# Query and key blocks of two attentions computed with tokens on partitions: head norms by VectorE sums in place of TensorE matmuls with ones

## The chip, the cores and the metric

The kernel runs on one core of a Trainium2 chip. The metric is the device time of one execution in microseconds (us); shorter is better. Five engines work side by side, each through its own queue of instructions: PE (TensorE), DVE (VectorE), ACT (ScalarE), POOL (GpSimd) and SP (SyncE, which issues the weight loads). They are ordered against each other by semaphores alone.

## The reference

Two transformer blocks on 256 tokens of width 2048, all in fp32. What the change touches lies in the first block:

```python
def rms_norm(x, g):
    y = xf * lax.rsqrt(jnp.mean(xf * xf, axis=-1, keepdims=True) + NORM_EPS)
    return y * g
...
h = rms_norm(x, norm_g)
proj = h @ w_in                                     # split into aq, ak, av, az, B's columns, cq, cz, ga, gb, gc
aq = rms_norm(aq.reshape(bsz, s, 8, 128), a_q_g)    # over each head's 128 channels
ak = rms_norm(ak.reshape(bsz, s, 8, 128), a_k_g)
ya = chunked_band_attention(aq, ak, av, a_rel_bias) * silu(az)
yb = rwkv7_time_mix(br, bk, bv, ...) * silu(bz)
m = rms_norm(mem, mem_norm_g)
mk, mv = split(m @ w_mem_kv)
mk = rms_norm(mk.reshape(bsz, 256, 4, 256), c_k_g)  # over each head's 256 channels
cq = rms_norm(cq.reshape(bsz, s, 4, 256), c_q_g)
yc = memory_cross_attention(cq, mk, mv) * silu(cz)
merged = sigmoid(ga) * (ya @ w_up_a) + sigmoid(gb) * (yb @ w_up_b) + sigmoid(gc) * (yc @ w_up_c)
x = x + merged @ w_o
```

Four tensors get a norm per head: `aq`, `ak` (8 heads of 128 channels), `cq`, `mk` (4 heads of 256). The second block has another attention, a gated linear attention, a short convolution and a feed-forward part; the change doesn't touch it.

## The kernel before

**Units.** All weights stream through a ring. A block is 512 output columns of a weight matrix (or four, three or one groups of 128), and is cut into units of 128x1024 weights (512 KB): for each unit SP loads `w_raw`, ACT rounds it to fp32r (`w_hi`, `hi`, L622), DVE takes the rest (`w_lo`, `lo`, L1002), and PE multiplies (`unit`, from L1547). Each product is three matmuls: hi by hi, lo by hi, hi by lo. `RING = 4` units are in flight, and ACT and DVE work `LEAD = 3` units ahead of PE: at the place of unit n they do unit n + 3, ACT after PE has finished unit n - 1 (`unit_used`).

**Kinds.** In a "wide" block the weights stand in the array and the tokens stream: a unit has 2 x 4 x 3 = 24 matmuls of 256 columns (L1582 to L1584), and the result has channels on partitions. In a "rows" block the tokens stand and the weights stream: 2 x 2 x 3 = 12 matmuls of 512 columns (L1573 to L1575), and the result has tokens on partitions. Both end in the same two PSUM banks of `gp`, from which `evacuate` copies (ACT, L622 to L690) or merges (DVE).

**Order.** `plan_stream` (from L49) sets the order of the blocks for all engines: lora, B0, B1, then B2 B3 A0 A1, A2 B4 B5 A3, B6 B7 A4 A5, A6 A7, one gate block, then gate_b, C, gate_a, mem, gate_c, up_c, o and the second block. A0 to A7 are the columns of aq (0, 1), ak (2, 3), av (4, 5), az (6, 7); C0, C1 those of cq; the first two blocks of mem those of mk. Between the steps of all other work each engine calls `fill(k)`, which runs the next k units. While the RWKV pairs are computed (`pairs(g)`, `pair_begin(p)`, four joint steps of two pairs each, PE's small matmuls at L1745) the filler is counted in quarters of a unit by the table `STEPS` (`planned_quarters` on PE). A quarter is six matmuls of a wide unit or three of a rows unit.

**Head norms.** `heads_norm` is called in gate_b after two units (for a_q, a_k), in gate_a after two (c_q), in gate_c after three (c_k). The tensors lie with channels on partitions, four of the eight 128-channel tiles being a half. For each half ACT squares 1024 elements a partition (L765); PE adds over the channels and spreads the sum by four fp32 matmuls with a matrix of ones into `psCD` (L1687); ACT takes the root from PSUM (`root`, L614); DVE has four (or two) reciprocals of 256 elements (L1130) and four multiplications by gain and reciprocal (L1133); PE goes on with 6 (or 3) units. Then the next half follows, in the same buffers. `attention` begins when its norms are done (`hn_done`).

```python
for t in range(4):
    hd = t // per_head
    ins = pe.matmul(psCD[:, hd * T:(hd + 1) * T], ones[:], buf[:, t * T:(t + 1) * T], ...)
```

**Transposes.** `turn_rows` (L1630) turns 128x512 by two token halves in eight 128x128 transposes with `ident` into one of two PSUM pairs `cross`; it is used for the norms of rows and for the merged branches (`up_and_project`).

Of the kernel before, what the change touches and what calls it, by code (L numbers as in the profile page):

```python
# [8 lines left out]
ALU = mybir.AluOpType  # L9
# [43 lines left out]
def plan_stream():  # L53
# [90 lines left out]
def plan_fill():  # L144

    upto, n = {}, 0
    for p in range(-1, KB // 2):
        for step, quarters in FIRST_STEPS if p < 0 else STEPS:
            n += quarters
            upto[p, step] = n  # L150
    return upto
CROSS = {"norm_g": 0, "merged": 4, "norm1_w_2": 8, "merged_2": 12, "norm2_w_2": 16, "ffn": 20}


def build(nc, dram, out):
# [9 lines left out]
    with ExitStack() as ctx:  # L165
# [37 lines left out]
        small = sb("small", [P, 32])  # L203
        y_ctx = ExitStack()
# [84 lines left out]
        hn_sq, hn_rs = area(64, UNIT), area(68, UNIT)  # L289
# [7 lines left out]
        cq_sq, cq_rs = area(0, UNIT), area(4, UNIT)  # L297
        c_sq, c_rs = area(48, UNIT), area(52, UNIT)
# [74 lines left out]
        def planned(unit):  # L373

            todo = list(range(units_of("B2")[0], units_of("gate_b0")[-1] + 1))

            def fill(p, step):
                while todo and todo[0] - first_todo < upto[p, step] // 4:
                    unit(todo.pop(0))

            def drain():
                while todo:
                    unit(todo.pop(0))
            first_todo = todo[0]
            fill.drain = drain
            return fill

# [220 lines left out]
        def _(act):  # L608
# [15 lines left out]
            def evacuate(m):  # L624
# [6 lines left out]
                tiles = g.rearrange("p (a b) -> p a b", b=T)  # L631
                if kind == "lora":
# [13 lines left out]
                elif kind == "a_cols":  # L646
                    if a in (4, 5):
                        act.activation(piece(a_v, a - 4), halves(g), ACT.Copy).then_inc(done, 1)
                    else:
                        dst = {0: a_q, 1: a_k, 3: a_z}[a // 2][:, 4 * (a % 2):4 * (a % 2) + 4, :]  # L650
                        act.activation(dst, tiles, ACT.Silu if a >= 6 else ACT.Copy).then_inc(done, 1)
                elif kind == "c_cols":
                    dst = (c_q, c_z)[a // 2][:, 4 * (a % 2):4 * (a % 2) + 4, :]
                    act.activation(dst, tiles, ACT.Silu if a >= 2 else ACT.Copy).then_inc(done, 1)
# [6 lines left out]
                elif kind == "mem":  # L661
                    if a >= 2:
                        act.activation(piece(c_v, a - 2), halves(g), ACT.Copy).then_inc(done, 1)
                    else:
                        act.activation(c_k[:, 4 * a:4 * a + 4, :], tiles, ACT.Copy).then_inc(done, 1)
# [92 lines left out]
            def heads_norm(src, size, buf, rs, fill, fills, ready=lambda half: None):  # L758

                for half in range(2):  # L760
                    ready(half)
                    if act_n["hn"]:
                        act.wait_ge(sem("hn_sq_used"), act_n["hn"])
                    act_n["hn"] += 1
                    act.activation(buf, src[:, 4 * half:4 * half + 4, :].rearrange("p a b -> p (a b)"), ACT.Square,  # L765
                                   scale=size ** -0.5).then_inc(sem("hn_sq"), 1)
                    act.wait_ge(sem("hn_sq_used"), act_n["hn"])
# [99 lines left out]
            for src in (a_q, a_k):  # L867
                heads_norm(src, 128, hn_sq, hn_rs, fill, 6)
# [6 lines left out]
            heads_norm(c_q, 256, cq_sq, cq_rs, fill, 3, lambda half: wait_evacuated(act, phases["C"][0] + half))  # L875
# [27 lines left out]
            heads_norm(c_k, 256, c_sq, c_rs, fill, 3, lambda half: wait_evacuated(act, phases["mem"][0] + half))  # L903
# [79 lines left out]
        def _(dve):  # L983
# [141 lines left out]
            def heads_norm(dst, gain, per_head, rs, fill, fills):  # L1125
                for half in range(2):
                    seen.need("root_ready")
                    for hd in range(4 // per_head):
                        r = rs[:, hd * T:(hd + 1) * T]
# [4 lines left out]
                        if hd == 4 // per_head - 1:  # L1134
                            ins.then_inc(sem("hn_done"), 1)
                        fill(1)
                    fill(fills - 4 // per_head)
# [235 lines left out]
            heads_norm(a_q, "a_q_g", 1, hn_rs, fill, 6)  # L1373
            heads_norm(a_k, "a_k_g", 1, hn_rs, fill, 6)
# [7 lines left out]
            heads_norm(c_q, "c_q_g", 2, cq_rs, fill, 3)  # L1382
# [34 lines left out]
            heads_norm(c_k, "c_k_g", 2, c_rs, fill, 3)  # L1417
# [122 lines left out]
        def _(pe):  # L1540
# [138 lines left out]
            def heads_norm(per_head, buf, fill, fills):  # L1679
                for _ in range(2):  # L1680
                    seen.need("hn_sq")
                    if pe_n["hn"]:
                        pe.wait_ge(sem("hn_done"), pe_n["hn"])
                    pe_n["hn"] += 1
# [193 lines left out]
            heads_norm(1, hn_sq, fill, 6)  # L1878
            heads_norm(1, hn_sq, fill, 6)
# [7 lines left out]
            heads_norm(2, cq_sq, fill, 3)  # L1887
# [11 lines left out]
            heads_norm(2, c_sq, fill, 3)  # L1899
# [95 lines left out]
```

## Time and profile before

| | us |
|---|---|
| median of 3 runs | 3014.78 (3014.73 to 3018.39) |
| profiled execution, its own time | 3016.61 |
| its span, first to last instruction | 3014.9 |
| PE busy | 2960.3 (98%) |
| DVE busy | 1643.0 (54%) |
| ACT busy | 1336.8 (44%) |
| mean share of the DMA queue with the weights | 56.9% |
| granted TensorE clock, mean | 0.995 of 2.4 GHz |

How to read it: a bar of PE lasts from issue to the modelled end of a pipelined matmul, and bars of successive matmuls overlap, so what a matmul costs is the distance between two starts. PE "busy" doesn't mean that the array is full. The chain that ended last is followed back from the end of the kernel, at each step to what released the instruction or to the one before it on its engine; its entries on PE are distances, and can be added.

### The profile page before, as it was taken

The numbers are of one execution on the slowest core, as the hardware profiler recorded it, in microseconds if no ns is written. First come the engines' busy times: TensorE is split into PE (matmuls) and PEld (weight loads), VectorE is DVE, ScalarE is ACT, GpSimd is POOL, SyncE is SP. The second block draws the span as 40 slices with busy tenths as digits, with TensorE's granted clock in tenths as the row PEclk, the third lists the DMA queues.
The fourth block names the chain that finished last, engine by engine and source line by source line (L and its number), as shares of the span: only waits on it lengthen the run. The fifth ranks groups of instructions, "written<-read, shape, count | busy, mean of one in ns | idle before, by whom it ended". The sixth has DMA issues, their size and how long they took to land.

```text
span 3014.9 us, 44248 instructions
## 1 busy us (share of the span) xinstructions
PE 2960.3 (98%) x18994; PEld 2546.8 (84%) x18994; DVE 1643.0 (54%) x1882; ACT 1336.8 (44%) x1522; POOL 68.7 (2%) x173
## 2 busy tenths in 40 slices
PE   7999999999999999999999999999999999999998
PEld 7999988889989888798998789888888888888886
DVE  4565665675656466454554466554654444444444
ACT  4452443454554454444454444444444444444333
POOL 4000000001000000000000000000000000000000
PEclk9999999999999999999999999999999999999999
DMA  7343444566665655656566555666556666666554
GB/s 205 112 135 113 138 130 119 154 187 182 212 196 180 177 152 190 188 161 181 168 173 197 151 147 164 190 185 191 192 175 191 182 185 184 183 187 196 188 188 147
DMA packets 356184, 518.40 MB, mean 172 GB/s; under 512 B 18288, under 2 KB 137220, under 8 KB 355220
## 3 DMA queue, kind: packets, MB, share of 16 engines
q1 hardware_dynamic: 355220, 512.37, 56.9%
q0 software_dynamic: 768, 3.20, 0.4%
q8 instruction: 149, 2.44, 0.3%
q14 instruction: 47, 0.39, 0.0%
HBM read 513.39 MB, written 2.11 MB: 171 GB/s over the span
## 4 chain that ended last, share of the span: by engine, by line
PE 94%; DVE 2%; ACT 1%; issue 1%; POOL 1%; DMA 0%; SPq 0%; DVEq 0%; POOLq 0%; ACTq 0%
PE gp L1573 21%; PE gp L1574 21%; PE gp L1575 21%; PE gp L1582 8%; PE gp L1584 8%; PE gp L1583 7%; PE ps L1745 4%; PE ps L1630 1%; PE ps L1702 1%; PE ps L1733 1%; DVE w_lo L1002 1%; PE ps L1687 0%; POOL m_work L518 0%; ACT w_hi L622 0%; DVE arena L996 0%
## 5 line engine op out<-in xcount | busy, mean ns | idle before, releaser
L1002 DVE TENSOR_TENSOR w_lo<-w_raw,w_hi 128x1024 fp32r<-128x1024 f32 (+2 forms) x976 | 1168.0, 1204 | 998.1 <-ACT w_hi L622 995.2
L622 ACT ACTIVATE w_hi<-w_raw 128x1024 fp32r<-128x1024 f32 (+2 forms) x976 | 1010.3, 1040 | 1183.2 <-PE gp L1575 892.8
L1573 PE MATMUL gp<-w_hi,h_hi 128*128 128x512 f32 x1920 | 764.9, 398 | 1.9 <-DVE w_lo L1002 1.4
L1574 PE MATMUL gp<-w_hi,h_lo 128*128 128x512 f32 x1920 | 758.4, 395 | 0.0
L1575 PE MATMUL gp<-w_lo,h_hi 128*128 128x512 f32 x1920 | 758.2, 395 | 0.0
L1582 PE MATMUL gp<-h_hi,w_hi 128*128 128x256 f32 x2080 | 601.5, 289 | 9.7 <-DVE w_lo L1002 7.4
L1583 PE MATMUL gp<-h_lo,w_hi 128*128 128x256 f32 x2080 | 581.7, 280 | 0.0
L1584 PE MATMUL gp<-h_hi,w_lo 128*128 128x256 f32 x2080 | 581.6, 280 | 0.0
L1573 PEld LDWEIGHTS gp<-w_hi,h_hi 128*128 128x128 f32 x1920 | 360.4, 188 | 88.7 <-DVE w_lo L1002 1.8
L1575 PEld LDWEIGHTS gp<-w_lo,h_hi 128*128 128x128 f32 x1920 | 360.3, 188 | 87.6
L1574 PEld LDWEIGHTS gp<-w_hi,h_lo 128*128 128x128 f32 x1920 | 360.5, 188 | 85.9 <-issue 0.2
L1582 PEld LDWEIGHTS gp<-h_hi,w_hi 128*128 128x128 f32 x2080 | 391.9, 188 | 20.2 <-DVE w_lo L1002 8.2
L1583 PEld LDWEIGHTS gp<-h_lo,w_hi 128*128 128x128 f32 x2080 | 392.2, 189 | 1.5 <-issue 0.7
L1584 PEld LDWEIGHTS gp<-h_hi,w_lo 128*128 128x128 f32 x2080 | 391.8, 188 | 0.0
L1573 PE MATMUL gp<-w_hi,y_hi 128*128 128x512 f32 x416 | 165.5, 398 | 0.0
L1575 PE MATMUL gp<-w_lo,y_hi 128*128 128x512 f32 x416 | 164.4, 395 | 0.0
L1574 PE MATMUL gp<-w_hi,y_lo 128*128 128x512 f32 x384 | 151.8, 395 | 0.0
L1573 PE MATMUL gp<-w_hi,f_hi 128*128 128x512 f32 x352 | 139.3, 396 | 0.0
L1574 PE MATMUL gp<-w_hi,f_lo 128*128 128x512 f32 x352 | 139.2, 395 | 0.0
L1575 PE MATMUL gp<-w_lo,f_hi 128*128 128x512 f32 x352 | 139.2, 395 | 0.0
L1745 PEld LDWEIGHTS ps<-arena 64*64 64x64 f32 x3072 | 104.5, 135 | 19.5 <-issue 4.9
L1745 PE MATMUL ps<-arena 64*64 64x32 f32 (+2 forms) x3072 | 116.4, 227 | 4.0 <-DVE arena L1235 4.0
(287 smaller groups left out, 1925.1 us busy)
## 6 DMA issues: line engine op xcount, KB each, us to landing
w_raw<-in_w_in SPq DMA_DIRECT2D x384, 512.0 KB, 3.8
w_raw<-in_w_ffn_gate SPq DMA_DIRECT2D x88, 512.0 KB, 4.4
w_raw<-in_w_ffn_up SPq DMA_DIRECT2D x88, 512.0 KB, 4.2
w_raw<-in_w_ffn_down SPq DMA_DIRECT2D x88, 512.0 KB, 4.1
w_raw<-in_w_in SPq DMA_DIRECT2D x136, 256.0 KB, 3.3
w_raw<-in_w_in SPq DMA_DIRECT2D x128, 192.0 KB, 3.1
w_raw<-in_w_mem_kv SPq DMA_DIRECT2D x32, 512.0 KB, 4.2
w_raw<-in_w_o SPq DMA_DIRECT2D x32, 512.0 KB, 4.2
```

What stands on the lines that cost most here:

```text
L622: act.activation(w_hi[:, slot, 0:size], w_raw[:, slot, 0:size], ACT.Copy).then_inc(sem("hi_done"), 1)
L1002: dve.tensor_tensor(w_lo[:, slot, 0:size], w_raw[:, slot, 0:size], w_hi[:, slot, 0:size].bitcast(F32), ALU.subtract)\
L1573: pe.matmul(o, xh, wh, start=(k == 0), stop=False)
L1574: pe.matmul(o, xl, wh, start=False, stop=False)
L1575: ins = pe.matmul(o, xh, wl, start=False, stop=(k == last_k))
L1582: pe.matmul(o, wh, x_hi[k], start=(k == 0 and c % 2 == 0), stop=False, skip_group_check=True)
L1583: pe.matmul(o, wh, x_lo[k], start=False, stop=False, skip_group_check=True)
L1584: ins = pe.matmul(o, wl, x_hi[k], start=False, stop=(k == last_k), skip_group_check=True)
L1630: ins = pe.transpose(cross[e % 2][:, c * T + a * P:c * T + (a + 1) * P], src[:, a, c * P:(c + 1) * P], ident[:])
L1702: ins = pe.matmul(ps[:, 2 + g % 2, tt * T + keys.start:tt * T + keys.stop], q[:, h * dt + d, tt * P:(tt + 1) * P], k[:, h * dt + d, 0:keys ...
L1733: ins = pe.matmul(psB[:, d * T + t0:(d + 1) * T], v[:, kt, at:at + P], pt[:, kt * T:(kt + 1) * T - t0], start=(kt == 0), stop=(kt == 1), s ...
L1745: ins = pe.matmul(out[hh], left[hh], right[hh], start=(i == 0), stop=(i == len(terms) - 1))
```

## The change

The blocks A0 to A3, C0, C1 and the first two of mem become rows blocks, so a_q, a_k, c_q and c_k arrive with tokens on partitions. Their evacuations on ACT put each head's 128 channels of a token half beside each other (`head_rows`). `heads_norm` is new on three engines and takes a whole list of tensors at once: ACT squares the halves into two buffers in turn; DVE sums each group of 128 squares (`tensor_reduce` into the new small tile `hn`, and for 256 channels one small add); ACT takes one root of all (32 or 8 columns); DVE takes one reciprocal and multiplies each half in place by its scales; PE turns each half back to channels on partitions by eight transposes into `cross`; ACT copies it from there with the gain as scale. The number of filler units in all is the same or nearly so: 2, 2 and 4 a step with four halves, 1, 1 and 2 with two.

```diff
+HN_FILL = {4: (2, 2, 4), 2: (1, 1, 2)}
...
-                phase(part, [Block("w_in", KD, "rows" if j in (4, 5) else "wide", A_COL + 512 * j, "h", "a_cols", j)])
+                phase(part, [Block("w_in", KD, "rows" if j < 6 else "wide", A_COL + 512 * j, "h", "a_cols", j)])
...
-    phase("C", wide("w_in", C_COL, 4, "h", "c_cols"))
+    phase("C", values(wide("w_in", C_COL, 4, "h", "c_cols"), 0, 1))
...
-    phase("mem", values(wide("w_mem_kv", 0, 4, "mem", "mem"), 2, 3))
+    phase("mem", values(wide("w_mem_kv", 0, 4, "mem", "mem"), 0, 1, 2, 3))
...
+        def head_rows(v, half):
+            return v[:, 4 * half:4 * half + 4, :].rearrange("p h (t c) -> p t h c", t=2)
...
+                    elif a < 4:
+                        act.activation(head_rows((a_q, a_k)[a // 2], a % 2), by_head, ACT.Copy).then_inc(done, 1)
...
@@ ACT
-                    act.activation(buf, src[:, 4 * half:4 * half + 4, :].rearrange("p a b -> p (a b)"), ACT.Square,
-                                   scale=size ** -0.5).then_inc(sem("hn_sq"), 1)
-                    act.wait_ge(sem("hn_sq_used"), act_n["hn"])
-                    if act_n["hn"] > 1:
-                        act.wait_ge(sem("hn_done"), act_n["hn"] - 1)
-                    w = UNIT * 128 // size
-                    root(rs[:, 0:w], psCD[:, 0:w])
-                    fill(fills)
+                for i, (v, half) in enumerate(halves):
+                    ready(i)
+                    if i >= 2:
+                        act.wait_ge(sem("hn_sum"), n0 + i - 1)
+                    act.activation(bufs[i % 2], tiles4(v, half), ACT.Square, scale=size ** -0.5).then_inc(sem("hn_sq"), 1)
+                    if i % 2:
+                        fill(HN_FILL[n][0])
+                act.wait_ge(sem("hn_sum"), n0 + n)
+                w = 8 * n // dt
+                root(hn[:, 0:w], hn[:, 0:w])
+                fill(HN_FILL[n][1])
+                for i, (v, half) in enumerate(halves):
+                    act.wait_ge(sem("hn_turned"), n0 + i + 1)
+                    for t in range(dt):
+                        dst = v[:, 4 * half:4 * half + 4, :].rearrange("p (a b) c -> p a b c", b=dt)[:, :, t, :]
+                        turned = cross[i % 2].rearrange("p (a b c) -> p a b c", b=dt, c=T)[:, :, t, :]
+                        ins = act.activation(dst, turned, ACT.Copy, scale=g2(gains[i // 2], t))
+                    ins.then_inc(sem("hn_done"), 1)
+                    fill(HN_FILL[n][2])
...
@@ DVE
-                        link(dve.reciprocal(r, r))
-                        for t in range(hd * per_head, (hd + 1) * per_head):
-                            v = dst[:, 4 * half + t, :]
-                            ins = dve.scalar_tensor_tensor(v, v, g2(gain, t % per_head), r, ALU.mult, ALU.mult)
...
+                for i in range(n):
+                    dve.wait_ge(sem("hn_sq"), n0 + i + 1)
+                    dve.tensor_reduce(means[:, 8 * i:8 * i + 8], bufs[i % 2].rearrange("p (a b) -> p a b", b=P), AX, ALU.add)\
+                        .then_inc(sem("hn_sum" if dt == 1 or i < n - 1 else "hn_parts"), 1)
+                    if i % 2 and i < n - 1:
+                        fill(HN_FILL[n][0])
...
+                fill(HN_FILL[n][0])
+                w = 8 * n // dt
+                inverse_root(hn[:, 0:w])
...
+                        ins = dve.tensor_tensor(part, part, scales.to_broadcast([P, 4 // dt, 2, P]), ALU.mult)
+                    ins.then_inc(sem("hn_scaled"), 1)
...
+                scaled(0)
+                scaled(1)
+                fill(HN_FILL[n][1])
+                for i in range(n):
+                    if 2 <= i + 1 < n:
+                        scaled(i + 1)
+                    fill(HN_FILL[n][2])
...
@@ PE
-                    for t in range(4):
-                        hd = t // per_head
-                        ins = pe.matmul(psCD[:, hd * T:(hd + 1) * T], ones[:], buf[:, t * T:(t + 1) * T],
-                                        start=(t % per_head == 0), stop=(t % per_head == per_head - 1))
-                    ins.then_inc(sem("hn_sq_used"), 1)
-                    fill(fills)
+                squares, middle, each_turn = HN_FILL[n]
+                fill(squares * n // 2 + middle)
+                for i, (v, half) in enumerate([(v, half) for v in srcs for half in range(2)]):
+                    pe.wait_ge(sem("hn_scaled"), n0 + i + 1)
+                    if i >= 2:
+                        pe.wait_ge(sem("hn_done"), n0 + i - 1)
+                    for j in range(4):
+                        for t in range(2):
+                            ins = pe.transpose(cross[i % 2][:, j * T + t * P:j * T + (t + 1) * P],
+                                               v[:, 4 * half + j, t * P:(t + 1) * P], ident[:])
+                    ins.then_inc(sem("hn_turned"), 1)
+                    fill(each_turn)
```

What this makes of the order is shown at gate_a, where the norm of c_q has the least filler around it. First PE, around the place where it enters the norm's first half; before:

```order
L1573 MATMUL gp<-w_hi,h_hi 128x512
L1574 MATMUL gp<-w_hi,h_lo 128x512
L1575 MATMUL gp<-w_lo,h_hi 128x512
L1687 MATMUL ps<-arena,ones 128x256 x4
L1573 MATMUL gp<-w_hi,h_hi 128x512
L1574 MATMUL gp<-w_hi,h_lo 128x512
L1575 MATMUL gp<-w_lo,h_hi 128x512
```

and now (L1616 to L1618 are the weight matmuls of before under their new line numbers):

```order
L1616 MATMUL gp<-w_hi,h_hi 128x512
L1617 MATMUL gp<-w_hi,h_lo 128x512
L1618 MATMUL gp<-w_lo,h_hi 128x512
L1733 MATMUL ps<-ident,arena 128x128 x8
L1616 MATMUL gp<-w_hi,h_hi 128x512
L1617 MATMUL gp<-w_hi,h_lo 128x512
L1618 MATMUL gp<-w_lo,h_hi 128x512
```

Four matmuls became eight transposes, and these stand two units later: behind four units of gate_a instead of two. Second, ACT from the square of the first half on, with the semaphores that each row waits for; before:

```order
L765 ACTIVATE arena<-arena 128x1024 [waits hn_sq_used,evacuated1]
L614 ACT_TABLE_LOAD [waits hn_done]
L614 ACTIVATE arena<-ps,small 128x512 [waits hn_sq_used]
L622 ACTIVATE w_hi<-w_raw 128x1024 [waits landed1,unit_used]
L622 ACTIVATE w_hi<-w_raw 128x1024 [waits landed2,unit_used]
L622 ACTIVATE w_hi<-w_raw 128x1024 [waits landed3,unit_used]
L765 ACTIVATE arena<-arena 128x1024 [waits hn_sq_used,evacuated0]
```

and now:

```order
L779 ACTIVATE arena<-arena 128x1024 [waits evacuated1]
L779 ACTIVATE arena<-arena 128x1024 [waits evacuated0]
L630 ACTIVATE w_hi<-w_raw 128x1024 [waits landed1,unit_used]
L622 ACT_TABLE_LOAD
L622 ACTIVATE hn<-hn,small 128x8 [waits hn_sum]
L630 ACTIVATE w_hi<-w_raw 128x1024 [waits landed2,unit_used]
L791 ACTIVATE arena<-ps,vec 128x2x256 [waits hn_turned]
L791 ACTIVATE arena<-ps,vec 128x2x256
L630 ACTIVATE w_hi<-w_raw 128x1024 [waits landed3,unit_used]
L630 ACTIVATE w_hi<-w_raw 128x1024 [waits landed0,unit_used]
```

Both squares stand in front of the next unit's rounding, one small root serves both halves, and a copy that waits for PE's transposes stands ahead of the rounding of later units. Third, DVE at the same place; before:

```order
L1130 RECIPROCAL arena<-arena 128x256 [waits root_ready]
L1133 SCALAR_TENSOR_TENSOR arena<-arena,vec 128x256 [waits dve_step]
L1133 SCALAR_TENSOR_TENSOR arena<-arena,vec 128x256
L1002 TENSOR_TENSOR w_lo<-w_raw,w_hi 128x1024 [waits hi_done]
L1130 RECIPROCAL arena<-arena 128x256
```

and now:

```order
L1153 TENSOR_REDUCE hn<-arena 128x8 [waits hn_sq] x2
L1160 TENSOR_TENSOR hn<-hn 128x8 [waits hn_parts]
L1022 TENSOR_TENSOR w_lo<-w_raw,w_hi 128x1024 [waits hi_done]
L1016 RECIPROCAL hn<-hn 128x8 [waits root_ready]
L1172 TENSOR_TENSOR arena<-arena,hn 128x2x256 [waits dve_step]
L1172 TENSOR_TENSOR arena<-arena,hn 128x2x256 x3
L1022 TENSOR_TENSOR w_lo<-w_raw,w_hi 128x1024 [waits hi_done] x7
```

DVE's part is now sums and multiplications in front of PE's step instead of reciprocals behind it.

## Rows read from the trace of the kernel before

**Rows 1.** Page of the whole span: busy time, and the chain by engine and line

```profile
PE 2960.3 (98%) x18994; PEld 2546.8 (84%) x18994; DVE 1643.0 (54%) x1882; ACT 1336.8 (44%) x1522; POOL 68.7 (2%) x173
...
PE 94%; DVE 2%; ACT 1%; issue 1%; POOL 1%; DMA 0%; SPq 0%; DVEq 0%; POOLq 0%; ACTq 0%
PE gp L1573 21%; PE gp L1574 21%; PE gp L1575 21%; PE gp L1582 8%; PE gp L1584 8%; PE gp L1583 7%; PE ps L1745 4%; PE ps L1630 1%; PE ps L1702 1%; PE ps L1733 1%; DVE w_lo L1002 1%; PE ps L1687 0%; POOL m_work L518 0%; ACT w_hi L622 0%; DVE arena L996 0%
```

**Rows 2.** Waits of PE over the span (us in total, times, longest us)

```profile
PE ps L1630 <- DVE arena L1080: 20.1, 3, 13.8
PE gp L1582 <- DVE w_lo L1002: 7.4, 4, 3.1
...
PE ps L1760 <- ACT arena L803: 0.5, 1, 0.5
```

**Rows 3.** ACT's timeline in two weight stretches (start us, us, operation [idle before])

```profile
1341.28 1.06 ACT L622 ACTIVATE w_hi<-w_raw 128x1024 fp32r<-128x1024 f32 x1 [1.77 <-PE gp L1584]
...
1355.41 1.06 ACT L622 ACTIVATE w_hi<-w_raw 128x1024 fp32r<-128x1024 f32 x1 [1.77 <-PE gp L1584]
...
2911.23 1.06 ACT L622 ACTIVATE w_hi<-w_raw 128x1024 fp32r<-128x1024 f32 x1 [1.74 <-PE gp L1575]
...
2939.23 1.06 ACT L622 ACTIVATE w_hi<-w_raw 128x1024 fp32r<-128x1024 f32 x1 [1.74 <-PE gp L1575]
```

**Rows 4.** PE's timeline around one sum of squares in gate_b

```profile
585.67 1.89 PE L1687 MATMUL ps<-arena,ones 128*128 128x256 f32 x8
587.21 0.58 PE L1573 MATMUL gp<-w_hi,y_hi 128*128 128x512 f32 x1
587.63 0.39 PE L1574 MATMUL gp<-w_hi,y_lo 128*128 128x512 f32 x1
```

**Rows 5.** PE's timeline around eight transposes in up_c

```profile
1158.53 1.03 PE L1630 MATMUL ps<-ident,arena 128*128 128x128 f32 x8
1159.32 0.48 PE L1573 MATMUL gp<-w_hi,y_hi 128*128 128x512 f32 x1
1159.64 0.40 PE L1574 MATMUL gp<-w_hi,y_lo 128*128 128x512 f32 x1
```

**Rows 6.** Groups by line and form: transposes (busy us, mean ns | idle)

```profile
L1630 PE MATMUL ps<-ident,f_t 128*128 128x128 f32 x88 | 11.4, 272 | 0.0
```

**Rows 7.** Chain in order of time: joint steps of the pairs (start us, us)

```profile
305.35 0.86 PE ps L1843 x2
...
345.38 2.82 PE ps L1745 x64
...
424.26 0.86 PE ps L1843 x2
...
463.33 2.83 PE ps L1745 x64
```

**Rows 8.** Gate_a from its third unit: ACT, DVE, and PE's entry of the chain

```profile
805.70 1.05 ACT L765 ACTIVATE arena<-arena 128x1024 f32<-128x1024 f32 x1
806.76 1.28 ACT L614 ACT_TABLE_LOAD   x1
...
805.82 1.23 DVE L1002 TENSOR_TENSOR w_lo<-w_raw,w_hi 128x1024 fp32r<-128x1024 f32 x1 [0.49 <-ACT w_hi L622]
...
807.49 1.73 PE ps L1687 x8
```

**Rows 9.** Groups by line and form: the nearest operations on DVE and ACT

```profile
L1130 DVE RECIPROCAL arena<-arena 128x256 f32<-128x256 f32 x24 | 42.0, 1748 | 18.6 <-ACT arena L614 18.6
...
L1157 DVE TENSOR_REDUCE small<-arena 128x1 f32<-128x256 f32 x24 | 9.6, 412 | 0.1
...
L1503 DVE TENSOR_TENSOR xr<-xr,gain 128x512 f32<-128x512 f32 x6 | 3.9, 684 | 0.0
L1168 DVE RECIPROCAL small<-small 128x2 f32<-128x2 f32 x20 | 3.2, 158 | 0.0
...
L614 ACT ACTIVATE stat<-stat,small 128x2 f32<-128x2 f32 x4 | 1.2, 295 | 1.1 <-DVE stat L1528 0.6 <-DVE stat L1074 0.5
```

More of the change, by code:

```diff
@@ L756, in _, with heads_norm @@
             act_n = Counter()
[L758 to L762, printed above, removed]
[L763 to L772 removed]
+            def heads_norm(srcs, gains, size, bufs, fill, ready=lambda i: None):
+                n0, n, dt = act_n["hn"], 2 * len(srcs), size // P
+                halves = [(v, half) for v in srcs for half in range(2)]
+                act_n["hn"] += n
+                for i, (v, half) in enumerate(halves):
[17 more added lines that the diff above has]
+                    fill(HN_FILL[n][2])
             def attention(which, n_heads, dt, fill, fills):
@@ L866, in _ @@
             fill(2)
-            for src in (a_q, a_k):
-                heads_norm(src, 128, hn_sq, hn_rs, fill, 6)
+            heads_norm([a_q, a_k], ["a_q_g", "a_k_g"], 128, hn_sq, fill)
             fill.drain()
@@ L874, in _ @@
             fill(2)
-            heads_norm(c_q, 256, cq_sq, cq_rs, fill, 3, lambda half: wait_evacuated(act, phases["C"][0] + half))
+            heads_norm([c_q], ["c_q_g"], 256, cq_sq, fill, lambda half: wait_evacuated(act, phases["C"][0] + half))
             for a in range(2):
@@ L902, in _ @@
             fill(3)
-            heads_norm(c_k, 256, c_sq, c_rs, fill, 3, lambda half: wait_evacuated(act, phases["mem"][0] + half))
+            heads_norm([c_k], ["c_k_g"], 256, c_sq, fill, lambda half: wait_evacuated(act, phases["mem"][0] + half))
             attention("c", 4, 2, fill, 6)
@@ L1123, in up_and_project, with heads_norm, scaled @@
                         dve.tensor_tensor(g_x[j], piece(xr, j), cols, ALU.mult).then_inc(sem("norm_rows"), 1)
[L1125 to L1129, printed above, removed]
-                        link(dve.reciprocal(r, r))
-                        for t in range(hd * per_head, (hd + 1) * per_head):
-                            v = dst[:, 4 * half + t, :]
-                            ins = dve.scalar_tensor_tensor(v, v, g2(gain, t % per_head), r, ALU.mult, ALU.mult)
[L1134 to L1137, printed above, removed]
+            def heads_norm(srcs, size, bufs, fill):
+                n0, n, dt = dve_n["hn"], 2 * len(srcs), size // P
+                halves = [(v, half) for v in srcs for half in range(2)]
+                dve_n["hn"] += n
+                means = hn[:, 0:8 * n] if dt == 1 else hn[:, 16:16 + 8 * n]
+                for i in range(n):
[4 more added lines that the diff above has]
+                        fill(HN_FILL[n][0])
+                if dt == 2:
+                    dve.wait_ge(sem("hn_parts"), n0 // 2 - 1)
+                    parts = means.rearrange("p (h d t) -> p h d t", d=2, t=2)
+                    dve.tensor_tensor(hn[:, 0:4 * n].rearrange("p (h t) -> p h t", t=2), parts[:, :, 0, :], parts[:, :, 1, :],
+                                      ALU.add).then_inc(sem("hn_sum"), 1)
+                fill(HN_FILL[n][0])
+                w = 8 * n // dt
+                inverse_root(hn[:, 0:w])
+                def scaled(i):
+                    v, half = halves[i]
+                    rows = v[:, 4 * half:4 * half + 4, :].rearrange("p (a b) (t c) -> p a b t c", b=dt, t=2)
+                    for d in range(dt):
+                        part = rows[:, :, d, :, :]
+                        scales = hn[:, i * w // n:(i + 1) * w // n].rearrange("p (a t) -> p a t", t=2).unsqueeze(3)
+                        ins = dve.tensor_tensor(part, part, scales.to_broadcast([P, 4 // dt, 2, P]), ALU.mult)
[7 more added lines that the diff above has]
+                    fill(HN_FILL[n][2])
@@ L1372, in _ @@
             fill(2)
-            heads_norm(a_q, "a_q_g", 1, hn_rs, fill, 6)
-            heads_norm(a_k, "a_k_g", 1, hn_rs, fill, 6)
+            heads_norm([a_q, a_k], 128, hn_sq, fill)
             fill.drain()
@@ L1381, in _ @@
             fill(2)
-            heads_norm(c_q, "c_q_g", 2, cq_rs, fill, 3)
+            heads_norm([c_q], 256, cq_sq, fill)
             fill(2)
@@ L1877, in _ @@
             fill(2)
-            heads_norm(1, hn_sq, fill, 6)
-            heads_norm(1, hn_sq, fill, 6)
+            heads_norm([a_q, a_k], fill)
             fill.drain()
@@ L1886, in _ @@
             fill(2)
-            heads_norm(2, cq_sq, fill, 3)
+            heads_norm([c_q], fill)
             fill(MEM_TURN_AT - 8)
@@ L1898, in _ @@
             fill(3)
-            heads_norm(2, c_sq, fill, 3)
+            heads_norm([c_k], fill)
             wait_evacuated(pe, phases["mem"][0] + 2)
```

29 lines of the change are left out of this document (14 added, 15 removed).

## The prediction

> **What bounds the kernel now.** The page comes first: TensorE is busy for 98% of the span, VectorE for 54%, ScalarE for 44%, and the chain that ended last is 94% PE, nearly all of it the weight matmuls of `unit` [rows 1]. So a microsecond of PE work taken out is a microsecond gained, unless a wait takes its place, and work of VectorE or ScalarE costs nothing until PE waits for it. Second, the waits of PE: the long ones stand at the start (norm rows, first weights), and only fragments are left for the rest [rows 2]. No line of the head norms is among them: in gate_b, gate_a and gate_c PE runs from unit to unit without a pause.
>
> Third, the pace of a unit. ScalarE's `hi` of a later unit starts when PE has finished one, so the distance between two such starts is one unit on PE. In a stretch of "wide" units (L1582 to L1584, 24 matmuls of 256 columns) six starts lie 1355.41 - 1341.28 = 14.13 us apart at five distances, 2.826 us a unit; in a stretch of "rows" units (L1573 to L1575, 12 matmuls of 512) eleven starts take 28.00 us, 2.800 us a unit [rows 3]. The bars of single matmuls (0.28 and 0.39 us) overlap and must not be multiplied.
>
> **The change, part by part.**
>
> *Sums of squares leave PE.* Each of eight halves (two of a_q, a_k, c_q, c_k) has four fp32 matmuls with `ones` at L1687, shown as eight records. The group starts at 585.67 and the next weight matmul at 587.21, and the one behind that comes 0.42 later where 2.800/12 = 0.233 is usual [rows 4]: 1.54 + 0.19 = 1.73 us, which is also the chain's entry for such a group [rows 8]. Removed: 8 x 1.73 = 13.8 us.
>
> *Transposes come in.* Each half now needs eight 128x128 transposes. The same eight stand in up_c: start 1158.53, next matmul 1159.32, the one behind it 0.32 later [rows 5], so 0.79 + 0.09 = 0.88 us. Added: 8 x 0.88 = 7.0 us. The difference is -6.8 us.
>
> Here a page speaks against the change. The single bar of a transpose is 272 ns [rows 6], but eight of them in a row advance PE by 0.88 us, 0.11 each [rows 5]; I count by the advance. The Trainium skill ("TensorE: Matmul & The Clock Gate", Part 4: PE-mode transpose) gives about 275 ns for a 128x128 transpose inside a kernel and says that the full clock does not engage for transposes. The bar agrees with that figure, and the advance does not follow it; were 275 ns paid for each, the 64 transposes would by estimate cost 17.6 us, more than the matmuls removed.
>
> *Eight blocks go from wide to rows.* A0 to A3, C0, C1 and the first two of mem, 8 units each: 64 x (2.826 - 2.800) = -1.7 us. For C and mem (32 units, -0.8) PE is the bound throughout. A0 to A3 are filler in the joint steps of the pairs, where a quarter goes from six to three matmuls. The trace has a comparison: from the bonus matmul (L1843) to the next products (L1745) the plan puts twelve units of filler. Between g = 1 and 2 this takes 345.38 - 305.35 = 40.03 us, with wide and pair units; between g = 2 and 3, where the filler is A4 and A5 (already rows), 463.33 - 424.26 = 39.07 us [rows 7]. Twelve units explain 12 x 0.026 = 0.3; the other 0.65 is a stall of the first case, the wait of L1760 for the square of ScalarE [rows 2]. By the plan the cover of that wait has some three units of A3 in it, now 0.03 us shorter each. I add 0.1 for it; were every saving of A0 to A3 turned into waiting, it would be 0.8, and that is this term's upper bound.
>
> *The wait for scaled rows.* This is the new dependency on PE's path: the first turn waits for `hn_scaled`, behind square, sum, root, reciprocal and multiply, and every later weight matmul is queued behind it. It is tightest in gate_a, where only two units cover it. ScalarE starts the square at 805.70 (1.05 us), then does the second, to 807.8. VectorE is free at 807.05 [rows 8]. A sum over 1024 elements is not in this trace. Its bounds: a two-input pass of 1024 takes 1.23 us [rows 8], and four times the 256-element reduction would be 1.65 us [rows 9]. I take 1.23, since four starts are not paid. So VectorE: 807.05 + 2 x 1.23 = 809.5, the small add 0.16 (as the small reciprocal [rows 9]), one `lo` of 1.23, to 810.9. ScalarE meanwhile: `hi` to 808.9, table load 1.28 to 810.1, small root 0.3 to 810.4 [rows 8, 9], so the root is ready before VectorE asks. Reciprocal 0.16, the two multiplies of the first half 2 x 0.68 [rows 9]: 812.4. PE comes to the turn two units behind 807.49, at 813.1 [rows 8]. That leaves 0.7 us, and the cost is nothing. With 1.65 for a reduction the multiply ends at 813.3 and PE waits 0.2; a stride that made the reductions and multiplies half as slow again (4 x 0.6) would make it 1.7. Gate_c has the same order, so the range of this term is 0 to about 3.4 us for the two. In gate_b six units cover the first turn, 16.8 us, and the same chain with twice the rows and two weight parts more ends some 4 us ahead of it: nothing.
>
> *The copy behind a turn.* ScalarE's copy waits for the transposes, and `hi` of a unit three ahead is queued behind it. Transposes, copy, `hi` and `lo` take 0.88 + 1.05 + 1.06 + 1.23 = 4.2 us from the turn's start [rows 5, 8], and PE needs that weight only after three units, 8.4 us. Nothing.
>
> *What is free.* VectorE loses 24 reciprocals of 1.75 us, 42 us [rows 9], and the multiplies with the gain; it gets eight sums and eight halves of multiplies, some 20 us. ScalarE swaps eight large roots for eight copies and three small roots. All of that lies beside PE, which waits for neither there [rows 2]; this relief therefore brings nothing either. The evacuations write the same number of elements in another order. GpSimd's bias loads wait for the fourth `hn_done`, which comes earlier now. SyncE's loads keep their order and wait only for `lo_done`.
>
> **Sum.** -13.8 + 7.0 - 1.7 + 0.1 = -8.4 us. The profiled execution took 3016.6 us and would take 3008.2. The median of the runs shown is 3014.8, 1.8 lower, so against it the forecast is 3006.4 us, 0.28% faster. A measurement of this kernel can tell about 0.2%, 6.0 us, from no change, so the margin is only 2.4 us.
>
> **The rivals.**
>
> *The saving turns into waiting.* Late first turns in gate_a and gate_c (up to 3.4) and no gain from A0 to A3 (0.7 more) leave -8.4 + 4.1 = -4.3: 3010.5 us, no change that can be told. For it: a margin of 0.7 us on a sum of eight durations. Against: each must be longer than its nearest row. 12%.
>
> *Transposes at their bar.* By 272 ns each [rows 6] 64 take 17.4 us instead of 7.0: +2.0 us in all, 3016.8, no change. It is the rule of the page above. Against it stands the advance of 0.88 us for eight [rows 5]. 2%.
>
> *The turn holds up the weights, and the kernel gets slower.* The place is ScalarE's copy behind `hn_turned` in gate_b, gate_a and gate_c. If ScalarE or VectorE is already late by more than 8.4 - 4.2 = 4.2 us when the turn comes (by a Sigmoid with its table load, or a merge that waits for its block), the weights run out and PE waits for `w_lo` at each of eight turns, copy, `hi` and `lo` uncovered: 8 x 3.3 = 27 us, so 3014.8 - 8.4 + 27 = 3033 us. Before the change ScalarE idles 1.74 us of each rows unit waiting for PE [rows 3], so it catches up such a delay within two or three units. 4%.
>
> **How the numbers follow.** The forecast has 80%, the first rival 12%, the page's 2%, the slower one 4%, and 2% is left for a cause that I don't see, on the slow side. Faster by over 0.2%: 0.80. Within: 0.14. Slower: 0.06. The range runs from 3004.4 (the 0.1 not paid and a scatter of 2 us, about the distance of the profiled execution to the median) to 3010.8, which takes in the first rival.
>
> **What would show it.** On the changed kernel's chain the entries of 1.73 us in gate_b, gate_a and gate_c are gone and eight of 0.87 us with x8 stand there; in gate_b a turn follows the one before by 4 x 2.80 + 0.88 = 12.1 us. The starts of `hi` in C0, C1 and the first mem blocks are 2.80 apart. Between g = 0 and 1 and between g = 1 and 2 the joint steps shrink by up to 0.3 us. PE's waits have no entry for the scaled rows over 0.3 us. I am wrong if PE waits in gate_a or gate_c for the multiply of VectorE for over a microsecond, if PE waits for `w_lo` behind a turn, or if a group of eight transposes advances PE by much more than 0.9 us.

## The result and the profile after

The changed kernel takes 2989.4 us (median of 4 runs, 2986.1 to 2990.6) against 3016.0 us beside it; the ratio is 0.9909, 95% interval 0.9892 to 0.9926. It is faster by 27 us, 0.9%, where the forecast was 8.4 us. The direction was right, the size off by a factor of three, and the time lies outside the range.

The page of the changed kernel, busy time and chain, beside [rows 1]:

```profile
PE 2935.4 (98%) x18226; PEld 2503.2 (84%) x18226; DVE 1609.5 (54%) x1851; ACT 1337.5 (45%) x1527; POOL 67.9 (2%) x173
...
PE 94%; DVE 2%; ACT 1%; issue 1%; POOL 1%; DMA 0%; SPq 0%; DVEq 0%; POOLq 0%; ACTq 0%
```

PE is the bound as before, and its chain share has not moved. So PE itself got through its work faster. First the parts that I had forecast. Chain in order of time, the eight turns of the head norms (start us, us):

```profile
601.37 0.87 PE ps L1733 x8
613.44 0.87 PE ps L1733 x8
...
807.30 0.87 PE ps L1733 x8
813.77 0.87 PE ps L1733 x8
```

Each costs 0.87 where a sum with ones cost 1.73, and between the first two lie 12.07 us = 4 x 2.80 + 0.87. DVE's timeline in gate_a ahead of the turn at 807.3:

```profile
801.17 2.34 DVE L1153 TENSOR_REDUCE hn<-arena 128x8 f32<-128x1024 f32 x2
803.54 0.17 DVE L1160 TENSOR_TENSOR hn<-hn 128x8 f32<-128x8 f32 x1
803.62 1.22 DVE L1022 TENSOR_TENSOR w_lo<-w_raw,w_hi 128x1024 fp32r<-128x1024 f32 x1
804.76 0.20 DVE L1016 RECIPROCAL hn<-hn 128x8 f32<-128x8 f32 x1
804.99 2.50 DVE L1172 TENSOR_TENSOR arena<-arena,hn 128x512 f32<-128x512 f32 x4
```

The two reductions take 1.17 each (I took 1.23), the first half is multiplied after two of the four rows of L1172, at about 806.2, and PE arrives about 1 us later. PE's waits have no entry for it.

Now what I had not forecast. ACT's timeline in ffn_down of the changed kernel, ten units apart, where [rows 3] has 28.00 us for ten:

```profile
2884.33 1.06 ACT L630 ACTIVATE w_hi<-w_raw 128x1024 fp32r<-128x1024 f32 x1 [1.66 <-PE gp L1618]
...
2911.53 1.06 ACT L630 ACTIVATE w_hi<-w_raw 128x1024 fp32r<-128x1024 f32 x1 [1.66 <-PE gp L1618]
```

27.20 us: a unit takes 2.720 instead of 2.800, in a stage 1.8 ms behind the last instruction that the change edits. The matmuls are the same, the clock is the same (mean 0.995 in both). Groups by line and form (busy us, mean ns) show which units these are; before the change all of these bars were 394 to 398 ns:

```profile
L1617 PE MATMUL gp<-w_hi,h_lo 128*128 128x512 f32 x2112 | 834.7, 395 | 0.0
...
L1617 PE MATMUL gp<-w_hi,y_lo 128*128 128x512 f32 x384 | 149.5, 389 | 0.0
...
L1617 PE MATMUL gp<-w_hi,f_lo 128*128 128x512 f32 x352 | 136.9, 389 | 0.0
...
L1617 PE MATMUL gp<-w_hi,mem_lo 128*128 128x512 f32 x128 | 49.8, 389 | 0.0
```

Units with h are as slow as ever, those with y, f and mem are fast. What separates them is where the tiles lie. The change allocates `hn`, 192 bytes a partition, behind h and ahead of y_hi, y_lo, mem and f. Its line is not among those of the diff shown ahead. The addresses in the two built programs (bytes in a partition; the distances follow from the shapes of the tiles as well):

```
            before    changed   distance to w_hi (32896), modulo 256: before, changed
h_hi         90304      90304                                     64,     64
y_hi, f_hi  127424     127616                                     64,      0
```

h_lo, y_lo, f_lo, mem_lo and mem_first lie whole multiples of 256 behind these, and w_lo behind w_hi.

### The profile page after: what moved, and what is told of

Its sections match the earlier page's. It is cut to its first block, busy times and chain, and to the rows that moved or that the text cites. A ratio compares the mean times of both kernels' runs of the same rounds, so it can differ in the third digit from the quotient of the medians.

```text
span 2988.1 us, 42670 instructions
## 1 busy us (share of the span) xinstructions
PE 2935.4 (98%) x18226; PEld 2503.2 (84%) x18226; DVE 1609.5 (54%) x1851; ACT 1337.5 (45%) x1527; POOL 67.9 (2%) x173
## 4 chain that ended last, share of the span: by engine, by line
PE 94%; DVE 2%; ACT 1%; issue 1%; POOL 1%; DMA 0%; SPq 0%; DVEq 0%; POOLq 0%; ACTq 0%
PE gp L1616 23%; PE gp L1618 23%; PE gp L1617 23%; PE gp L1625 6%; PE gp L1626 6%; PE gp L1627 6%; PE ps L1791 4%; PE ps L1673 1%; PE ps L1748 1%; PE ps L1779 1%; DVE w_lo L1022 1%; POOL m_work L526 0%; ACT w_hi L630 0%; DVE arena L1016 0%; PE ps L1769 0%
## 5 line engine op out<-in xcount | busy, mean ns | idle before, releaser
L1616 PE MATMUL gp<-w_hi,h_hi 128*128 128x512 f32 x2112 | 845.2, 400 | 1.9 <-DVE w_lo L1022 1.4
L1617 PE MATMUL gp<-w_hi,h_lo 128*128 128x512 f32 x2112 | 834.7, 395 | 0.0
L1618 PE MATMUL gp<-w_lo,h_hi 128*128 128x512 f32 x2112 | 834.6, 395 | 0.0
L1625 PE MATMUL gp<-h_hi,w_hi 128*128 128x256 f32 x1696 | 490.7, 289 | 8.9 <-DVE w_lo L1022 6.1
L1616 PEld LDWEIGHTS gp<-w_hi,h_hi 128*128 128x128 f32 x2112 | 396.8, 188 | 96.9 <-DVE w_lo L1022 1.8
L1618 PEld LDWEIGHTS gp<-w_lo,h_hi 128*128 128x128 f32 x2112 | 396.7, 188 | 96.0
L1626 PE MATMUL gp<-h_lo,w_hi 128*128 128x256 f32 x1696 | 475.4, 280 | 0.0
L1627 PE MATMUL gp<-h_hi,w_lo 128*128 128x256 f32 x1696 | 475.0, 280 | 0.0
L1625 PEld LDWEIGHTS gp<-h_hi,w_hi 128*128 128x128 f32 x1696 | 320.5, 189 | 17.5 <-DVE w_lo L1022 6.9
L1626 PEld LDWEIGHTS gp<-h_lo,w_hi 128*128 128x128 f32 x1696 | 320.6, 189 | 1.1 <-issue 0.5
L1627 PEld LDWEIGHTS gp<-h_hi,w_lo 128*128 128x128 f32 x1696 | 320.1, 189 | 0.0
L1616 PE MATMUL gp<-w_hi,y_hi 128*128 128x512 f32 x448 | 175.2, 391 | 0.0
L1618 PE MATMUL gp<-w_lo,y_hi 128*128 128x512 f32 x448 | 174.5, 390 | 0.0
L1616 PE MATMUL gp<-w_hi,f_hi 128*128 128x512 f32 x352 | 137.0, 389 | 0.0
L1618 PE MATMUL gp<-w_lo,f_hi 128*128 128x512 f32 x352 | 136.9, 389 | 0.0
```

The lines of the kernel that those rows point to most:

```text
L1616: pe.matmul(o, xh, wh, start=(k == 0), stop=False)
L1617: pe.matmul(o, xl, wh, start=False, stop=False)
L1618: ins = pe.matmul(o, xh, wl, start=False, stop=(k == last_k))
L1625: pe.matmul(o, wh, x_hi[k], start=(k == 0 and c % 2 == 0), stop=False, skip_group_check=True)
L1626: pe.matmul(o, wh, x_lo[k], start=False, stop=False, skip_group_check=True)
L1627: ins = pe.matmul(o, wl, x_hi[k], start=False, stop=(k == last_k), skip_group_check=True)
```

## The experiments

In each run the pace of a unit is read from the starts of matmuls in the second block. A rows unit has 12 matmuls, so 2.800 us a unit is 233.3 ns from one start to the next, and 2.720 us is 226.7 ns.

**The tile alone, and the work alone.** The kernel before with only an unused tile:

```diff
         small = sb("small", [P, 32])
+        pad = sb("pad", [P, 48])
```

> The kernel before with nothing but an unused tile of 192 bytes a partition in front of y_hi, where the change puts hn. Theory A (place in memory): rows units whose standing operand lies behind it (y_hi, y_lo, mem, f_hi, f_lo; 200 units here) go from 2.800 to 2.720 us, h units stay at 2.800, wide units at 2.826: 200 x 0.08 = 16 us less, about 3000 us. Rival B (the faster units come from the change's own work, such as less load on VectorE and SBUF): every unit keeps 2.800, time as before, 3016 us.

Measured: 3001.9 us, ratio 0.9953 (0.9938 to 0.9968). PE's timeline of this kernel in ffn_down, thirty matmuls apart:

```profile
2849.79 0.39 PE L1575 MATMUL gp<-w_hi,f_lo 128*128 128x512 f32 x1
...
2856.59 0.39 PE L1575 MATMUL gp<-w_hi,f_lo 128*128 128x512 f32 x1
```

6.80 us for thirty, 226.7 ns each. An unused tile makes the kernel 15 us faster; rival B is out, as the cause of the faster units. The counterpart keeps all of the change's work and takes the shift away:

```diff
-        hn = sb("hn", [P, 48])
...
         arena = sb("arena", [P, ARENA], F32, y_ctx)
+        hn = sb("hn", [P, 48], F32, y_ctx)
```

> The changed kernel with hn behind the arena, so that y_hi, y_lo, mem, f_hi and f_lo lie where they lay before; all of its work is kept. Theory A: all rows units are back at 2.800 us, and what is left is the change's own work, my -8.4 us: about 3007.5 us. Rival B: it keeps the whole gain, about 2989 us.

Measured: 3006.2 us, ratio 0.9966 (0.9955 to 0.9978); ffn_down is back at 7.00 us for thirty matmuls, 233.3 ns:

```profile
2849.77 0.40 PE L1618 MATMUL gp<-w_lo,f_hi 128*128 128x512 f32 x1
...
2856.77 0.40 PE L1618 MATMUL gp<-w_lo,f_hi 128*128 128x512 f32 x1
```

So the work of the change is worth 11 us (7 to 14) and the place of the tiles the rest, 15 us by the first run and 17 by the second.

**Which property of the place.** Two runs moved h too.

```diff
# shift_h
-        stat = sb("stat", [P, 16])
+        stat = sb("stat", [P, 32])
# shift_both: this, and
-        hn = sb("hn", [P, 48])
+        hn = sb("hn", [P, 64])
```

> The changed kernel with 64 bytes a partition more in stat, in front of h_hi. All tiles behind move by 64: h_hi to a multiple of 128 bytes, y_hi and f_hi to an odd multiple of 64. Theory A with the step 128 bytes: the 528 rows units with h go to 2.720 (-42 us), the 216 with y, mem and f go back to 2.800 (+17 us): about 2964 us. Rival (only the distance to w_hi counts, which is 128 above a multiple of 256 as y_hi in the changed kernel, and h_hi now is not): no unit is fast, about 3007 us.

> The changed kernel with 64 bytes more in stat and 64 more in hn: h_hi and y_hi both on multiples of 128 (and of 256) bytes. Theory A with the step 128 bytes: all 744 rows units at 2.720 us, about 2989 - 42 = 2947 us. Rival (distance to w_hi modulo 256): none is fast, about 3007 us. Wide units (the h tile streams there, the weights stand) stay at 2.826 if only the standing operand's place counts, and get faster if the streaming one's counts too.

Measured: 3003.8 us (0.9959, 0.9944 to 0.9974) and 3005.8 us (0.9963, 0.9950 to 0.9976). Both kernels lost the fast units, so my theory of 128-byte boundaries fell, and the rival written beside it held: h in both, and y in the second, now lie 128 from a multiple of 256 behind w_hi. Their matmuls are 232.3 ns apart, nearly as slow as before. PE's timeline of shift_h, thirty matmuls apart:

```profile
2649.78 0.39 PE L1617 MATMUL gp<-w_hi,h_lo 128*128 128x512 f32 x1
...
2656.75 0.39 PE L1617 MATMUL gp<-w_hi,h_lo 128*128 128x512 f32 x1
```

The new theory C: the distance between the two operands of a matmul decides, modulo 256 or 512 bytes. The best case for it costs no memory, since without `stat` h_hi starts 57344 bytes behind the start of w_hi, a multiple of 512:

```diff
-        stat = sb("stat", [P, 16])
         h_hi = sb("h_hi", [P, KD, T], F32R)
         h_lo = sb("h_lo", [P, KD, T], F32R)
+        stat = sb("stat", [P, 16])
```

> The changed kernel with the tile stat behind h_lo instead of ahead of h_hi; no tile behind it moves. h_hi then starts 57344 bytes behind w_hi, a multiple of 512, as y_hi does (94720 bytes) in the changed kernel; before it was 57408. Theory C (the distance of the two operands decides: a multiple of 256 or 512 gives 226.7 ns for a 512-column matmul and 120.0 ns for a 256-column one, an odd multiple of 64 gives 233.3 and 117.7, 128 gives 232.3 and 119.7): the 528 rows units with h gain 12 x 6.65 ns = 0.080 us each, -42 us; the 212 wide, pair and trio units lose up to 24 x 2.3 ns each, +10 us: about 2958 us. Rival D (the absolute place decides: only 128 above a multiple of 256 is fast): h_hi now is on an even 128 (90240 = 705 x 128, 128 above a multiple of 256), the same forecast; the next run tells C from D.

Measured: 2959.5 us, ratio 0.9810 (0.9793 to 0.9826), 58 us faster than the kernel before and 30 faster than the changed one. The matmuls with h:

```profile
2649.81 0.39 PE L1617 MATMUL gp<-w_hi,h_lo 128*128 128x512 f32 x1
...
2656.61 0.39 PE L1617 MATMUL gp<-w_hi,h_lo 128*128 128x512 f32 x1
```

226.7 ns. This is the version that beats both kernels. Its price stands in the wide units, where the h tile streams. ACT's starts in Q of this kernel, three units in 8.64 us, 2.880 each where [rows 3] has 2.826:

```profile
1344.85 1.06 ACT L630 ACTIVATE w_hi<-w_raw 128x1024 fp32r<-128x1024 f32 x1 [1.82 <-PE gp L1627]
...
1353.49 1.06 ACT L630 ACTIVATE w_hi<-w_raw 128x1024 fp32r<-128x1024 f32 x1 [1.82 <-PE gp L1627]
```

**Distance or absolute place.** All tiles moved by the same 64 bytes:

```diff
+        lead = sb("lead", [P, 16])
         w_raw = sb("w_raw", [P, RING, UNIT])
```

> The changed kernel with an unused tile of 64 bytes ahead of w_raw: every tile moves by 64 bytes, every distance stays. Theory C (distance decides): units as in the changed kernel, y, mem and f rows units at 2.720 us, about 2989 us. Rival D (absolute place decides, y_hi now on an odd multiple of 64): they go to 2.80 us, about 3006 us.

Measured: 2989.6 us (0.9910, 0.9895 to 0.9925), the changed kernel's time; its matmuls with f are still 226.7 ns apart, those with h 233.3. The absolute place is out. The other way round, only the weight ring moves (with xr and gain):

```diff
+        stat = sb("stat", [P, 16])
         w_raw = sb("w_raw", [P, RING, UNIT])
...
-        stat = sb("stat", [P, 16])
```

> The changed kernel with stat ahead of w_raw: w_hi and w_lo move up by 64 bytes, and h_hi, h_lo, y_hi, y_lo, mem, f_hi and f_lo stay exactly where they are in the changed kernel. Theory C (distance of the two operands modulo 256): h units become fast although h did not move (528 x 0.080 = -42, wide units +12), y, mem and f units become slow (+17): about 2976 us. If the place of the standing operand alone decided, the time would stay at 2989 us.

Measured, one execution: 2968.5 us. Matmuls with h are 226.7 ns apart although h_hi stayed at 90304, so the distance is what counts. But y and f did not go to 233.3; at a distance of 192 modulo 256 their thirty matmuls take 6.86 us, 228.7 ns:

```profile
2849.72 0.39 PE L1617 MATMUL gp<-w_hi,f_lo 128*128 128x512 f32 x1
...
2856.58 0.39 PE L1617 MATMUL gp<-w_hi,f_lo 128*128 128x512 f32 x1
```

That is 216 x 12 x 4.6 ns = 12 us better than I expected, and explains the difference to 2976 but for some 4 us the other way. "An odd multiple of 64 is slow" was too coarse: 64 is slow, 192 only a little.

**The period and the step.** The changed kernel with a longer hn:

```diff
-        hn = sb("hn", [P, 48])
+        hn = sb("hn", [P, 112])    # y_by_256
+        hn = sb("hn", [P, 56])     # y_by_32
```

> The changed kernel with hn 256 bytes longer: y, mem and f lie 94976 bytes behind w_hi, an odd multiple of 256. If the pattern repeats every 256 bytes: their rows matmuls stay 226.7 ns apart and the time is that of the changed kernel, about 2989 us. If it repeats only every 512: they go to 232 to 233 ns, about 3005 us.

> The changed kernel with hn 32 bytes longer: y, mem and f lie 32 bytes off the multiple of 512. If the pattern is of 64-byte pieces, a start in the same piece keeps 226.7 ns (2989 us); if any shift counts, 233 ns and about 3005 us.

Measured, one execution each: 2990.0 and 3006.1 us; 226.7 and 233.3 ns. The pattern repeats after 256 bytes, and 32 bytes are already as bad as 64. Together, for matmuls of 512 columns with 128x128 standing, by the distance from w_hi to the tile with the tokens (h, y, mem or f), modulo 256:

```
distance     0     32     64    128    192
ns       226.7  233.3  233.3  232.3  228.7
```

**Other traffic in the memory.** A rival of the two operands was not tried in a run: ScalarE, VectorE and the weight loads write into w_hi, w_lo and w_raw while PE reads a tile with tokens, and those three lie multiples of 256 from each other, so they keep the same distance to it. The traces settle it. At the end of ffn_down no load and no instruction of another engine is left beside PE. Thirty matmuls there, before and changed (us, busy time and count of PE, PEld, DVE, ACT, POOL, then the granted clock, the share of DMA and GB/s):

```profile
2996.20:3003.20 7.00, 7.00 (x32) 5.64 (x30) 0.00 (x0) 0.00 (x0) 0.00 (x0) 1.00 0.00 0
...
2969.59:2976.39 6.80, 6.80 (x32) 5.63 (x30) 0.00 (x0) 0.00 (x0) 0.00 (x0) 1.00 0.00 0
```

With everything else at rest it is 233.3 ns against 226.7 again. So the difference lies in what PE itself does.

**The change's own work in the better layout.** The kernel before, placed as stat_behind is:

```diff
-        stat = sb("stat", [P, 16])
...
         h_lo = sb("h_lo", [P, KD, T], F32R)
+        stat = sb("stat", [P, 16])
...
         small = sb("small", [P, 32])
+        pad = sb("pad", [P, 48])
```

> The kernel before, its work untouched, with stat behind h_lo and an unused 192 bytes ahead of y_hi: h_hi, y_hi, mem and f lie at the addresses that they have in the run stat_behind. Theory C: rows units 2.720 us, wide units about 2.885 us. Against the kernel before 480 rows units with h and 200 with y, mem and f gain 0.080 each (-54 us) and 276 wide, pair and trio units lose 0.06 each (+16): about 2979 us. Against stat_behind (2959.5) it then lacks the change's own work, now 7 us of PE matmuls and 64 units at 2.885 - 2.720 = 0.165 us (10.6): some 17.5 us more, 2977 us. If the places alone were the whole gain, it would be at 2959 us. In the stage of the gated linear attention both profiles without the change's work had a weight load of 4.25 us on the chain and all with it 2.8 us: if that goes with the program, it stands here at 4.25 again.

Measured: 2977.9 us, ratio 0.9876 (0.9859 to 0.9892). 39 us come from the place alone, with no edit to any instruction. The change's work is worth 18.4 us here, the distance of this median to that of stat_behind; that is, as expected, more than the 11 in the old layout, because a wide unit now costs 0.16 us more than a rows unit instead of 0.026. The weight load in the stage of the gated linear attention did not stand at 4.25 us again:

```profile
1806.62 2.99 DMA w_raw<-in_w_in
```

**The price of a turn.** Every transpose of the norms twice:

```diff
-                    for j in range(4):
+                    for j in (0, 1, 2, 3, 0, 1, 2, 3):
```

> The changed kernel with every transpose of heads_norm made twice (64 more, the same values written again). By the distance of starts in the trace 64 transposes cost 7.0 us of PE: a turn advances PE by about 1.75 us, in all 2996 us. By their bar of 272 ns each (the rival of the prediction) 17.4 us: 3006 us.

Chain of this kernel:

```profile
601.35 1.75 PE ps L1733 x16
...
810.77 1.75 PE ps L1733 x16
```

A turn of 16 advances PE by 1.75 us, 0.109 us a transpose. One execution took 2999.4 us, 10 more than the changed kernel; 7.0 of them are there by gate_c (attention begins at 1055.50 instead of 1048.54). Another 2.3 arise at the entry of Q and are not the price of a transpose. From the last rows unit ahead of Q to the end of its eighth unit, in the changed kernel and in this one:

```profile
1264.80:1298.03 33.23, 28.09 (x226) 27.27 (x225) 21.71 (x24) 13.88 (x17) 4.46 (x7) 0.95 0.44 125
...
1271.76:1307.26 35.50, 30.36 (x226) 29.59 (x224) 21.70 (x24) 13.88 (x17) 4.46 (x7) 0.86 0.42 121
```

The work is the same, but the mean granted clock is 0.86 instead of 0.95: the clock falls to half (1.2 GHz) while PE waits for the norm, and is back after 3.4 us in the changed kernel's trace, ahead of the first matmul of Q, but in this one only after 10.2 us, some 4 us into Q. It stood at half for 10.2 us there in the traces of shift_both, y_by_256, y_by_32 and before_placed too, none of which has more transposes. The Trainium skill ("TensorE: Matmul & The Clock Gate", Part 4: PE-mode transpose) gives about 275 ns inside a kernel, for bf16: the bar agrees with it (272 ns [rows 6]), the advance in a row does not. Nor did the clock fall for transposes here: it is 1.00 from 595 to 645 us of the changed kernel, where four of its turns stand.

**The cover of the turn.** One unit less ahead of the first turn, and one more behind each, where two halves are normed:

```diff
-HN_FILL = {4: (2, 2, 4), 2: (1, 1, 2)}
+HN_FILL = {4: (2, 2, 4), 2: (1, 0, 3)}
```

> The changed kernel with one unit instead of two between the norm's entry and the first turn in gate_a and gate_c (and three instead of two units behind each turn). In the changed kernel the first multiply is done about 0.9 us ahead of the turn in gate_a. If the wait for the scaled rows is what I take it for, PE now waits 2.8 - 0.9 = 1.9 us in each of the two places, +3.8 us: about 2993 us. If the turn is not bound to that chain, 2989 us.

Measured, one execution: 2992.1 us. PE's waits have the new entry (us, times, longest):

```profile
PE ps L1733 <- DVE arena L1172: 3.7, 2, 1.9
```

Twice 1.9 us, as computed from the margin. The wait for the scaled rows is real, and the change's schedule just covers it. The span of this profile is only 2.3 us longer than the changed kernel's (2990.4 against 2988.1), so the wait is shown by its entry, and less well by the whole time.

## Why the prediction was wrong, point by point

*What bounds the kernel:* right. PE was the bound before and after, and a microsecond less of PE was a microsecond gained.

*Sums leave, transposes come:* right. 1.73 became 0.87 for each of eight halves, -6.9 us.

*Eight blocks to rows, -1.7 with 0.1 back:* right in the old layout. From the first to the second group of pairs the products' starts come 0.8 us closer, from the second to the third 0.3, the third to the fourth none: 1.1 for A0 to A3 where 0.7 was forecast. The stall of L1760 stayed (0.6 us). In the layout that the change in fact makes, the 16 mem units gain 0.08 more each.

*The wait for scaled rows, the copy behind a turn:* right, 0 us. The sum of eight durations put the first half at 812.4 against a turn at 813.1, a margin of 0.7, and the trace has about 1. One bound beside it was added up wrongly: two reductions and two multiplies, half as slow again, are 2 x 0.6 + 2 x 0.34 = 1.9 us more and not 2.4, so the wait would be 1.2 and not 1.7, and the range of the term 0 to 2.4. The first rival would then stand at 3.1 us and not 4.1. The measured time lies far from both.

*What is free:* right that the relief of DVE brings nothing.

*The sum, -8.4:* for the work alone the runs give -11.0, with an interval (-7 to -14) that holds it. By the traces, the unshifted kernel is ahead by 7.7 us when the gated linear attention starts, close to the forecast, and by 10.6 when it ends. The chain of the kernel before, then that of the unshifted one:

```profile
1739.31 1.23 PE ps L1937 x4
...
1812.84 4.25 DMA w_raw<-in_w_in
...
1819.83 0.97 PE ps L1937 x4
...
1881.41 0.88 PE ps L1960 x4
```

```profile
1731.57 1.22 PE ps L1982 x4
...
1805.25 2.79 DMA w_raw<-in_w_in
...
1810.77 0.70 PE ps L1982 x4
...
1870.78 0.88 PE ps L2005 x4
```

I had no term for these 2.9 us. Half of them, 1.5, is one weight load that PE waits for, 4.25 us in one kernel and 2.79 in the other. The other half is TensorE's clock behind that wait. The stretch from there to the next transposes, before and unshifted:

```profile
1819.83:1844.43 24.60, 24.60 (x189) 23.54 (x190) 12.67 (x20) 11.08 (x14) 0.00 (x0) 0.93 0.51 139
...
1810.77:1833.80 23.03, 23.03 (x189) 22.23 (x190) 12.67 (x20) 11.92 (x15) 0.00 (x0) 1.00 0.60 163
```

The same 189 matmuls take 1.6 us more at a mean granted clock of 0.93: in the kernel before the clock stood at half for 3.4 us, after PE had waited for 1.9 us; in the unshifted one it stayed at 1.00. Neither goes simply with the change's work. The load took 4.27 with the unused tile, where no such fall of the clock followed, and 2.99 in the placed kernel before; what sets them stays open. By these two profiles, then, some 3 us of the difference belong to none of the forecast's terms.

*The step that failed* is the third of the reading: "a 'rows' unit 2.800 us". I read the pace of a unit as a property of its kind and let 680 units of the kernel keep it, and I priced every instruction of the change but not its one allocation. The new tile moves five operands by 192 bytes, from 64 to 0 modulo 256 behind w_hi, and 216 rows units go from 2.800 to 2.720 us: 17.3 us. With the 8.4 that makes 25.7 of the 27 measured; that the sum comes so near is in part luck, since the work alone measured 11. The sentence on evacuations and queues that "keep their order" asked what moves in time and never what moves in memory.

The rivals: none of mine was it. The saving did not turn into waiting, transposes were not paid at their bar, no turn held up the weights. The 2% for "a cause that I don't see" I had put on the slow side, without a reason. The direction was no luck: without the shift the kernel is still faster by 11 us.

## What to carry to other kernels

A new tile is an edit to every tile allocated behind it: compare the addresses of matmul operands in the two programs before pricing anything else, and when a stage that the change doesn't touch gets faster or slower, pad the old kernel by the same bytes first. A difference of 2 or 3 us that arises at one place can be the granted clock: compare it over the same matmuls before giving it to the edit. Where PE is the bound, try the allocation order as a parameter of its own; here moving a 64-byte tile behind its neighbour gave more than the whole rewrite of the norms. Measure both kinds of matmul, since the place that helps 512 streaming columns hurt those of 256.

## What the hardware showed that I had not expected

The spacing of back-to-back fp32r matmuls with a new 128x128 standing operand each depends on where the two operands lie to each other. With 512 columns it is 226.7 ns at a distance of 0 modulo 256 bytes and 228.7 to 233.3 ns at the others tried; with 256 columns it is 117.7 ns at 64 (2.826 us for 24) and 120.0 at 0 (2.880 us). The common shift of all tiles changes nothing. Moving tiles alone took 39 us (1.3%) off the kernel before and 30 us (1.0%) off the changed one. The Trainium skill ("SBUF — State Buffer", Operand start alignment) asks only for a start at a multiple of the element size and says that this is about legality and not speed; these runs show that speed is another matter.

Why it is so isn't shown. It is not other traffic (233.3 and 226.7 ns with every other engine and the DMA at rest). The bars of the weight loads are 188 ns at either distance, so it is not seen there. Whether it is the standing and the streaming operand of one matmul that meet, or the streaming one and the next weight load, wasn't tried in a run. The changed kernel's trace has a hint where units with y (distance 0) and with h (64) follow each other: from the last matmul with y to the first with h it took 225 or 226 ns all 15 times, and the other way 229 to 236. The next weight load alone would have it the other way round. Distances in steps below 32 bytes and other types weren't tried. At a distance of 128 the wide units in Q took 2.85 us in one kernel and 2.88 in the other with the same addresses of h and w, and this stays open too.
